# Expert outputs times their gates, added in memory by the storing DMA; the last stage reads two sums per token

## What is computed

```python
scores = sigmoid(xt @ w_router)                       # (1032, 64)
# biased scores pick 4 of 8 groups, then the top 6 experts of each token
w = take_along_axis(scores, eidx, axis=1)
w = w / sum(w, axis=-1, keepdims=True) * 2.5          # six gates per token
routed[token] += gate * ((silu(x @ Wg[e]) * (x @ Wu[e])) @ Wd[e])   # for each of its six experts e
y = x1 + gate_f * (routed + shared_expert(x))
```

## Time and profile before

| | before |
|---|---|
| median of 3 runs | 2876.22 us (2875.36 to 2877.65) |
| the profiled execution | 2880.32 us |
| its span | 2878.5 us |
| granted TensorE clock, mean share of full speed | 0.945 |
| busy: TensorE, VectorE, ScalarE, GpSimd | 89%, 52%, 38%, 13% |
| `stage_routed`, first gate-up matmul to last eviction | 1993.95 to 2771.71 |
| `stage_combine` | 2778.02 to the end |

### The profile page before, as it was taken

The page is one execution under the profiler, slowest core; times in us unless marked ns, Lnnn a source line. Parts: engine busy times, 40 slices in busy tenths (PEclk is TensorE's granted clock), DMA queues, the critical chain, the costliest instruction groups (busy, mean ns, idle before and its releaser), DMA issues. The chain is left out here.

```text
span 2878.5 us, 44074 instructions
## 1 busy us (share of the span) xinstructions
PE 2562.8 (89%) x14550; PEld 1472.2 (51%) x14550; DVE 1508.7 (52%) x3758; ACT 1106.2 (38%) x2384; POOL 374.8 (13%) x419
## 2 busy tenths in 40 slices
PE   6998995979989899986889869797999999999977
PEld 2444443558878687874566634344333333333332
DVE  1556554658878688785888564584111111111126
ACT  1223212659878698773655401221111111111110
POOL 0000001011010010101232031052000000000035
PEclk8999996979999899987999989898999999999988
DMA  8122168422173120207100083216989898897867
GB/s 333 47 64 80 41 198 304 140 100 74 41 256 107 56 74 23 88 1 191 35 26 18 17 285 117 104 37 273 410 329 420 318 359 337 314 386 269 314 244 279
DMA packets 192864, 511.69 MB, mean 178 GB/s; under 512 B 24169, under 2 KB 102315, under 8 KB 160440
## 3 DMA queue, kind: packets, MB, share of 16 engines
q1 hardware_dynamic: 139932, 318.07, 30.9%
q0 software_dynamic: 28640, 127.09, 12.3%
q10 hardware_dynamic: 24132, 64.49, 5.9%
HBM read 631.86 MB, written 86.93 MB: 250 GB/s over the span
## 5 line engine op out<-in xcount | busy, mean ns | idle before, releaser
L3015 PE MATMUL routed_ex_pG<-dispatch_exWG,routed_ex_XT 128*64 128x512 f32 x2048 | 452.1, 598 | 13.9 <-DMA dispatch_exWG<-in_w_e_gu 12.0
L2138 DVE TENSOR_REDUCE ssqc<-SQ 128x8 f32<-128x512 f32 x516 | 346.1, 683 | 116.9 <-ACT SQ L1941 102.1
L1846 PE MATMUL eK<-dWkv,LT 128*128 128x256 f32 x1032 | 316.4, 389 | 12.6 <-ACT SQ L1941 12.3
L1849 PE MATMUL eK<-WA,LT 128*128 128x272 f32 x1032 | 326.7, 399 | 0.0
L1941 ACT ACTIVATE SQ<-eK 128x512 f32<-128x512 f32 x516 | 292.2, 602 | 56.2 <-PE eK L1849 41.2
L3015 PEld LDWEIGHTS routed_ex_pG<-dispatch_exWG,routed_ex_XT 128*64 128x64 f32 x2048 | 147.6, 138 | 313.1 <-issue 312.7
L3106 DVE TENSOR_TENSOR routed_ex_sg<-routed_ex_sg,routed_ex_pG 128x256 f32<-128x256 f32 x64 | 27.0, 422 | 528.4 <-ACT routed_ex_sg L3063 528.4
L3034 PE MATMUL routed_ex_pY<-routed_ex_WD,routed_ex_AT 128*64 128x512 f32 x1024 | 233.8, 598 | 1.0 <-DMA routed_ex_WD<-in_w_e_down 0.9
L1849 PEld LDWEIGHTS eK<-WA,LT 128*128 128x128 f32 x1032 | 200.7, 195 | 28.8 <-DVE numc L2137 0.3
L1846 PEld LDWEIGHTS eK<-dWkv,LT 128*128 128x128 f32 x1032 | 189.4, 195 | 48.0 <-ACT SQ L1941 17.3
L3063 ACT ACTIVATE routed_ex_sg<-routed_ex_pG 128x256 f32<-128x256 f32 x64 | 24.5, 383 | 448.2 <-PE routed_ex_pG L3015 448.2
(11 more groups left out here) (562 smaller groups left out, 3884.5 us busy)
## 6 DMA issues: line engine op xcount, KB each, us to landing
dispatch_exWG<-in_w_e_gu SPq DMA_DIRECT2D x256, 1024.0 KB
routed_ex_WD<-in_w_e_down SPq DMA_DIRECT2D x132, 1024.0 KB, 11.0
s_yblk<-routed_ex_Y ACTq DMA_DIRECT2D x64, 512.0 KB
ada_Win<-in_w_ada ACTq DMA_DIRECT2D x8, 2048.0 KB, 8.7
s_yblk<-zrows SPq DMA_DIRECT2D x15, 1024.0 KB, 14.4
ada_Wada<-in_w_ada SPq DMA_DIRECT2D x8, 1024.0 KB, 11.7
...
```

The source lines that it names most:

```text
L1846: pe.matmul(pK[kn % 3][:, 512 + z:512 + z + HK], key, Wkv[:, 4:8, 0:NOPE], start=True, stop=True)
L1849: pe.matmul(pK[kn % 3][:, z:z + HK + 16], key, WA[:, pr, :], start=True, stop=True).then_inc(s_KN, 1)
L2138: dve.tensor_reduce(ssqc[cg % 2][:, n - 1 - tau, :], SQ[kn % 4].rearrange("p (h d) -> p h d", h=H), AX.X, ALU.add).then_inc(s_red, 1)
L3015: m = pe.matmul(pG[u][r, :], XT[u][:, k, r], WG[2 * u + v][:, k, :], start=(k == 0), stop=(k == KD - 1))
```

## The change

The store of a block becomes an indirect DMA that GpSimd issues, with addition in memory: row r of the block is added to the row of its token in `yblk`. The two groups of a block may hold the same token, so there are two sums per token: partitions 0 to 63 add to rows from 0, partitions 64 to 127 to rows from `LANE1`; rows without a token add to spare rows. A block's rows are scaled by their gate in ScalarE's eviction. For that the gates are stored to memory as a table of 64 per token (in the unused `x1`), the row of each token is gathered beside its activations, and VectorE keeps only the column of the group's own expert. An add waits until the add before has landed. The zero fill covers the 19 blocks of sums. The combine stage loads two plain tiles, adds them and goes on as before, with ScalarE issuing the stores.

```diff
+LANE1, SPARE = (NT + 1) * P, 2 * (NT + 1) * P
...
@@ stage_prompt @@
-    full = 2 * -(-NTOK * TK // (4 * GRP))
-    spans = [(b, min(b + 2, NBLK)) for b in range(full, NBLK, 2)]
+    spans = [(b, min(b + 3, SPARE // P + 1)) for b in range(0, SPARE // P + 1, 3)]
...
@@ the table of gates @@
+def gate_rows(T):
+    return T["x1"].rearrange("a b -> (a b)").rearrange("(n e) -> n e", e=NE)[0:(NT + 1) * P, :]
...
@@ stage_dispatch, SyncE: ahead of the expert numbers, and at the end @@
+            sp.wait_ge(s_gt, 1)
+            sp.dma_start(gate_rows(T).rearrange("(t p) e -> p t e", p=P), GT[:, :, :]).then_inc(s_gts, 16)
+            sp.wait_ge(s_gts, 16)
...
@@ stage_dispatch, VectorE, after the lists are built @@
-            for k in range(TK):
-                link(dve.tensor_tensor(S2[:, :, :], SV[:, :, :], slotf[:, :, k:k + 1].to_broadcast(sh), ALU.is_equal))
-                link(dve.tensor_tensor(S2[:, :, :], S2[:, :, :], GT[:, :, :], ALU.mult))
-                link(dve.tensor_reduce(G["gate"][:, :, k], S2[:, :, :], AX.X, ALU.add))
-            link(dve.tensor_scalar(place[:, :, :], place[:, :, :], 0.0, None, ALU.max))
-            link(dve.tensor_copy(G["slot"][:, :, :], place[:, :, :]))
+            link(dve.tensor_copy(G["begin"][:, :], start[:, :]))
+            link(dve.tensor_copy(G["reach"][:, :], be[:, :]))
+            link(dve.tensor_scalar(away[:, 0:1], c("half32"), 1.0 / 16.0, None, ALU.mult))
+            link(dve.tensor_tensor(G["group"][:, 0:1], away[:, 0:1], nq[:, :], ALU.mult))
+            link(dve.scalar_tensor_tensor(out=G["group"][:, 1:2], in0=nq[:, :], scalar=2.0, in1=G["group"][:, 0:1], op0=ALU.mult, op1=ALU.add))
+            link(dve.tensor_scalar(away[:, 1:2], c("part"), float(SPARE), None, ALU.add))
+            link(dve.tensor_scalar(away[:, 0:1], away[:, 0:1], float(LANE1), -1.0, ALU.mult, ALU.add))
+            link(dve.tensor_tensor(away[:, 0:1], away[:, 0:1], away[:, 1:2], ALU.subtract))
+            link(dve.memset(G["list"][:, NBLK:NBLK + 2], 0))
-            link(dve.memset(G["list"][:, NBLK:NBLK + 2], 0))
-            link(dve.tensor_copy(G["list"][:, 0:NBLK], pL))
+            link(dve.tensor_scalar(G["list"][:, 0:NBLK], pL, -1.0, 0.0, ALU.add, ALU.max))
+            link(dve.tensor_scalar(used[:, :], pL, 0.5, None, ALU.is_ge))
+            link(dve.scalar_tensor_tensor(out=used[:, :], in0=pL, scalar=away[:, 0:1], in1=used[:, :], op0=ALU.add, op1=ALU.mult))
+            link(dve.tensor_scalar(G["to"][:, :], used[:, :], away[:, 1:2], None, ALU.add))
...
@@ stage_routed, GpSimd @@
                                         in_offset=bass.IndirectOffsetOnAxis(ap=ix[b][:, 0:1], axis=0)).then_inc(s_x[b], 16)
+                pool.indirect_dma_start(out=GR[b][:, :], out_offset=None, in_=gate_rows(T),
+                                        in_offset=bass.IndirectOffsetOnAxis(ap=ix[b][:, 0:1], axis=0)).then_inc(s_g[b], 16)
+
+            def add_rows(i, q):
+                for u in range(2):
+                    pool.wait_ge(s_st[1 - u], (i * 2 + q) * 16 + (16 + 16 * u))
+                    pool.tensor_copy(iy[u][:, :], G["to"][:, bass.ds(i * 4 + (2 * q + u), 1)]).then_inc(s_iy, 1)
+                    pool.wait_ge(s_iy, i * 4 + (2 * q + u + 1))
+                    pool.wait_ge(s_ye, i * 8 + (4 * q + 2 * u + 2 + 2))
+                    pool.sem_inc(s_k, 1)
+                    pool.indirect_dma_start(out=out[0:SPARE + P, :], out_offset=bass.IndirectOffsetOnAxis(ap=iy[u][:, 0:1], axis=0), in_=Y[u][:, :],
+                                            in_offset=None, compute_op=ALU.add).then_inc(s_st[u], 16)
+
+            def pair(i, q):
+                gather_next(i, q)
+                add_rows(i, q)
             def gather_next(i, q):
                 for u in range(2):
                     b, ahead = 2 * (1 - q) + u, 2 * q + 2 + u
                     pool.wait_ge(s_xt, i * 8 + (2 * ahead + 1))
+                    pool.wait_ge(s_gc, i * 4 + (2 * q + 1))
                     pool.tensor_copy(ix[b][:, :], G["list"][:, bass.ds(i * 4 + ahead, 1)]).then_inc(s_ix, 1)
                     pool.wait_ge(s_ix, i * 4 + (ahead + 1))
                     pool.sem_inc(s_k, 1)
...
                 pool.wait_ge(s_ix, u + 1)
                 pool.sem_inc(s_k, 1)
                 fetch(u)
-            run(pool, gather_next)
+                pool.indirect_dma_start(out=Y[u][:, :], out_offset=None, in_=T["h2"],
+                                        in_offset=bass.IndirectOffsetOnAxis(ap=ix[u][:, 0:1], axis=0)).then_inc(s_st[u], 16)
+            run(pool, pair)
...
@@ stage_routed, ScalarE @@
-            for u in range(2):
-                act.dma_start(T["pad"][u:u + 1, :], c("iota")[0:1, :]).then_inc(s_st[u], 16)
-                    act.activation(Y[u][:, n * 512:(n + 1) * 512], pY[n][:, :], ACT.Copy).then_inc(s_ye, 1)
+                        act.wait_ge(s_gc, n0 + u + 1 + 1)
+                    act.activation(Y[u][:, n * 512:(n + 1) * 512], pY[n][:, :], ACT.Copy, scale=gate[u][:, 0:1]).then_inc(s_ye, 1)
-                for u in range(2):
-                    act.wait_ge(s_ye, (n0 + u) * 2 + 2 + 2)
-                    act.dma_start(out.rearrange("(t p) d -> t p d", p=P)[bass.ds(n0 + u, 1)].rearrange("a p d -> p (a d)"),
-                                  Y[u][:, :]).then_inc(s_st[u], 16)
...
@@ stage_routed, VectorE @@
                     dve.tensor_tensor(av[u][:, :], sg[u][:, :], pG[u][:, DE:2 * DE], ALU.mult).then_inc(s_a, 1)
+                def gates(u):
+                    b, at = 2 * q + u, 3 * (2 * q + u)
+                    dve.wait_ge(s_g[b], i * 16 + 16)
+                    dve.wait_ge(s_gv, i * 12 + (at + 1))
+                    dve.scalar_tensor_tensor(out=gs[u][:, :], in0=reach[:, :], scalar=group[:, u:u + 1], in1=GR[b][:, :],
+                                             op0=ALU.is_gt, op1=ALU.mult).then_inc(s_gv, 1)
+                    dve.wait_ge(s_gv, i * 12 + (at + 2))
+                    dve.scalar_tensor_tensor(out=gs[u][:, :], in0=begin[:, :], scalar=group[:, u:u + 1], in1=gs[u][:, :],
+                                             op0=ALU.is_le, op1=ALU.mult).then_inc(s_gv, 1)
+                    dve.wait_ge(s_gv, i * 12 + (at + 3))
+                    dve.tensor_scalar(group[:, u:u + 1], group[:, u:u + 1], 1.0, None, ALU.add).then_inc(s_gv, 1)
+                    dve.wait_ge(s_ye, i * 8 + (4 * q + 2 * u + 1))
+                    dve.tensor_reduce(gate[u][:, :], gs[u][:, :], AX.X, ALU.add).then_inc(s_gc, 1)
                 for u in range(2):
+                    gates(u)
                     for n in range(2):
...
@@ stage_combine, the new lines @@
+    NR = 4
+    E = [[sb(f"cE{i}{v}", [P, D]) for v in range(2)] for i in range(NR)]
+    s_m, s_v, s_e, s_z, s_o = sem("cb_m"), sem("cb_v"), [sem(f"cb_e{i}") for i in range(NR)], sem("cb_z"), sem("cb_o")
+                if t >= NR:
+                    sp.wait_ge(s_z, t - NR + 1)
+                for v, first in enumerate((0, LANE1)):
+                    sp.dma_start(E[t % NR][v][0:R, :], T["yblk"][first + t * P:first + t * P + R, :]).then_inc(s_e[t % NR], 16)
+                if t == 0:
+                    sp.dma_start(gf[:, :], T["mod"][NS:NC9, 5 * D:6 * D].to_broadcast([P, D])).then_inc(s_m, 16)
+                    sp.dma_start(gfs[:, :], T["mod"][0:NS, 5 * D:6 * D]).then_inc(s_m, 16)
+                act.wait_ge(s_z, t + 1)
+                act.dma_start(token_rows(y_p, y_s, t), z[0:R, t, :]).then_inc(s_o, 16)
+            act.wait_ge(s_o, 16 * (NT + 1))
+                a, b = (e[0:R, :] for e in E[t % NR])
+                dve.wait_ge(s_e[t % NR], 32 * (t // NR + 1))
+                link(dve.tensor_tensor(a, a, b, ALU.add))
+                if t == 0:
+                    dve.wait_ge(s_m, 32)
+                link(dve.tensor_tensor(a, a, gf[0:R, :] if t < NT else gfs[:, :], ALU.mult))
```

More of the change, by code:

```diff
@@ L163, in build @@
         G["lg"] = sb("lg", [P, NT + 1, NE])
-        G["gate"] = sb("gate", [P, NT + 1, TK])
-        G["slot"] = sb("slot", [P, NT + 1, 8], I32)
         G["expert"] = sb("expert", [5, P], I32)
@@ L187, in build @@
             if st is stage_dispatch:
+                for n, w, dt in (("reach", NE, F32), ("begin", NE, F32), ("group", 2, F32), ("to", NBLK, I32)):
+                    G[n] = root.enter_context(nc.sbuf_tensor(n, [P, w], dt, side="right"))
                 weights_ex = root.enter_context(ExitStack())
@@ L2579, in stage_dispatch @@
     tokf = sb("gtokf", [P, NTT])
+    start, away, used = sb("gstart", [P, NE]), sb("gaway", [P, 2]), sb("gused", [P, NBLK])
     slotf, posf, blkf = (sb("g" + n, [P, NTT, 8]) for n in ("slotf", "posf", "blkf"))
@@ L2777, in _ @@
             link(dve.tensor_scalar(tokf[:, :], c("iota")[:, 0:NTT], float(P), c("part"), ALU.mult, ALU.add))
+            link(dve.tensor_scalar(tokf[:, :], tokf[:, :], 1.0, None, ALU.add))
             dve.wait_ge(s_in, 16)
@@ L2851, in _ @@
             link(dve.tensor_tensor(nb[:, :], be[:, :], nb[:, :], ALU.subtract))
```

(1 more changed line is left out.)

65 lines of the change are left out of this document (9 added, 56 removed).

## The result

The changed kernel takes **3021.16 us** (median of 4 runs, 3015.49 to 3026.01) against 2875.79 for the kernel before on the same chip: ratio 1.0508, 95% interval 1.0494 to 1.0522. It is 5.1% slower, where +14 us and a range of 2840 to 2980 were forecast. The profiled execution has a span of 3024.1 us, 145.6 above the 2878.5 of before.

A forecast was written before the change was run, and what follows sets the result against it. TensorE was taken as the bound, with the DMA engines close behind. Combine -59, head +3, routed stage +66 and tail +4 gave +14 us on 2876.2, so 2890 us, range 2840 to 2980.

The forecast's parts named there:

- rival (a): Routed stage: gathers behind the adds come late, so TensorE pays in full and middle pairs, +6 to +60 us; chance 0.45.
- the fixed "8.6" of the loop: GpSimd's loop in the routed stage: 8.6 us per turn besides the landings of one add and one gather.
- Light pairs: 8.6 + 5.8 + 4.5 + 0.7 = 19.6, nothing: Routed stage, 7 pairs with gathers of 4.6 us or less: a 19.6 us loop, hidden by TensorE's 23.56, costs nothing.
- the 26.4 of middle pairs: Routed stage, 11 pairs with gathers between light and full: loop of 26.4 us, +2.8 us each, 31 us in all.
- a pair of 30 isn't full any more. I take 28.5: Routed stage, 12 full pairs: 30 us by the loop, 27 by the engines, taken as 28.5; +35 us in all.
- The unknown A: Routed stage: an add's time from issue to landing, taken as the gather's plus 1.3 us, for twice the reading.
- Rival (c): Routed stage: adds are slow, rows read and written one after the other, +97 us to 2973 or more; chance 0.15.
- Rival (b): GpSimd's loop: the adds hide behind TensorE, about +20 us in the routed stage, -32 in all, 2844 us; chance 0.32.
- Combine: Combine stage: plain loads replace gathers and VectorE sets the pace, 3.66 us per tile; 41 us for 100.5, -59.
- Head: Start of the routed stage: GpSimd's extra issues delay the second block's rows, +3 us (0 to 5).
- Tail: Last eviction to combine stage: the last two adds land one after the other, +4 us (+1 to +10).
- Demand: DMA engines, routed stage: 3.35 us more per pair, from 1.30 us per add's second read and at most 0.75 for gate rows.

The follow-up runs named there:

- x3_noload: The changed kernel with the reloading of expert weights left out for all experts but one of the 64; 2816.07 us, 0.9791 of the kernel before.
- x1_plain: The changed kernel with the storing DMA writing to the same rows instead of adding; 2907.61 us, 1.0112 of the kernel before.
- x1_warm: The changed kernel with ten dummy 128x512 matmuls before TensorE's wait for the gathered rows; 3096.09 us, 1.0756 of the kernel before.

## Why the prediction was wrong

**The mechanism** was right: the gathers behind the adds, new waits of the transposes on gathered rows, weight waits gone. This was rival (a), with a price 120 us too low. Its own sum, laid on the pair shown above (a full one), beside x3_noload; its last figure is a sum, since TensorE sets the pair there:

| term, us | forecast, full pair | measured | without weight loads |
|---|---|---|---|
| transposes to the first add's issue | 5.6 | 8.11 | 6.19 |
| add, issue to landing (A) | 10.1 | 10.37 | 6.67 |
| landing to the gather's issue | 3.0 | 3.72 | 3.70 |
| gather to the transposes (G and what is ahead of it) | 11.3 | 11.65 | 5.0 |
| turn | 30.0 | 33.85 | 21.6 |

One full pair flatters the forecast. The same terms for 30 turns of the changed kernel, in the prediction's three kinds (by what the gathers of the same pair took before the change), forecast and measured mean:

| kind | to the add's issue | A | landing to gather's issue | G | turn |
|---|---|---|---|---|---|
| 12 full | 5.6, 8.4 | 10.1, 9.5 | 3.0, 3.7 | 11.3, 10.4 | 28.5, 32.0 |
| 11 middle | 5.6, 8.5 | 8.8, 6.9 | 3.0, 3.8 | 9.0, 10.5 | 26.4, 29.7 |
| 7 light | 5.6, 7.6 | 5.8, 6.6 | 3.0, 3.9 | 5.2, 10.8 | 23.6, 28.9 |

**The step that failed, and the larger part: the fixed "8.6" of the loop.** It measured 12.0 us in the mean, which over 30 turns is 101 us. 57 of them are the clock (2.1 us in each of 27 pairs): nothing in the sum said what TensorE does after idling. The trace before had waits for weights with slower matmuls behind them, and the forecast named the lower clock in its first part and then priced it at nothing. The rest is 0.6 us a turn up to the add's issue, there without any wait too (6.19 in x3_noload), and 0.8 behind its landing, most of it the issue of an add, 1.6 us for 0.96.

**The second step: "Light pairs: 8.6 + 5.8 + 4.5 + 0.7 = 19.6, nothing", and with it the 26.4 of middle pairs.** Light pairs took 28.9. The forecast carried over how long a gather had taken in each kind of pair, but the change also moved the gather to another place in the pair. A light pair, the one of the middle line of the earlier trace rows: the windows of its turn in the changed kernel (transposes to add, add, second add, gather), then the issues of gate-up weights and gather there, and before:

```profile
2362.80:2372.00 9.20, 9.20 (x36) 4.47 (x38) 2.68 (x7) 1.65 (x3) 0.00 (x1) 0.66 0.08 23
2372.00:2379.10 7.10, 7.10 (x36) 2.33 (x34) 0.84 (x2) 1.37 (x2) 1.63 (x2) 1.00 0.82 222
2379.10:2382.80 3.70, 3.70 (x20) 1.25 (x18) 0.03 (x1) 0.38 (x1) 1.98 (x4) 1.00 0.62 186
2382.80:2392.60 9.80, 6.73 (x32) 2.17 (x28) 2.46 (x8) 0.77 (x2) 4.29 (x6) 1.00 1.03 339
...
2379.53 10.78 SPq L2968 DMA_DIRECT2D dispatch_exWG<-in_w_e_gu  x8
2382.78 1.03 POOL L2983 DMA_INDIRECT routed_ex_X<-s_h,routed_ex_ix  x1 [0.83 <-POOL routed_ex_ix L3007]
```

```profile
2279.57 8.82 SPq L2945 DMA_DIRECT2D dispatch_exWG<-in_w_e_gu  x8
2290.17 0.96 POOL L2960 DMA_INDIRECT routed_ex_X<-s_h,routed_ex_ix  x1 [0.79 <-POOL routed_ex_ix L2967]
```

Before, the gather went out 10.6 us behind the first gate-up load (10.8 in the median of the pairs), after the change 3.2 (3.2 in the median): in the middle of the loads. The engines are full for these 10 us and nearly idle for the 9 before the add, so the gather lands as in a full window though the pair is light. The same holds for "a pair of 30 isn't full any more. I take 28.5": full pairs took 32.0. The middle pair's window had a share of 0.98 besides; the forecast went by its 361 GB/s. In all, 27 of 31 distances were long, their mean 30.3 (before 24.3).

Over the 30 turns the two fixed terms are +101 us, G +45 and A -22; 10 us come off, since the forecast took 23.6 for light pairs where its own loop gave 19.6, and 28.5 for full ones where it gave 30.0. That leaves 115 of the 120; the last turn and the rounding of the terms give the rest.

**The unknown A** was well placed, even a little high: the first adds landed in 7.0 us in the median (6.2 to 10.7), 9.5 in the mean of full pairs for 10.1; the second adds, whose landing is not in this chain, in 10.1. The step that A stood on, "twice the reading", holds with 1.46 to 1.57 us of the engines' time against 1.30. Rival (c), rows one after the other, falls with the 6.4 us of x3_noload and with these landings; its sign "every pair long, light ones too" came all the same, for another reason, and that its 2973 came near the result is chance. Rival (b) would have come with idle engines, as in x3_noload. The rule of the Trainium skill that was weighed beside it (page "DMA: Bandwidth & Descriptors", section "Anatomy of one DMA — SWDGE (gpsimd) path") gave 3.2 us for a gather and 4.4 for an add. The trace doesn't agree: 5.0 and 6.4 without the weight loads, 11.6 and 7.0 (median of the first adds) with them.

**Combine:** the pace is 2992.12 - 2987.38 at the first tile and 2995.78 - 2992.12 = 3.66 us behind it, as worked out from the earlier trace rows; 41.65 against 41. **Dispatch:** nothing, as forecast; the 3.9 us in the first row of the table are no part of the change, since x1_plain, with the same stages up to there, ends dispatch at 1979.34, and x1_warm, also with the same, at 1985.11. **Head:** +4.7 for +3; the second block's wait is 9.20 for 4.51. **Tail:** +9.7 for +4. The second add went out 1.07 us behind the first's landing, as forecast, but from its issue to the combine stage it took 12.7 us where 8.1 was put. **Demand:** 36.8 us are left with the ring opened. The "at most 0.75 us" of the gate rows holds with 0.33.
